# Bounded gathers and dealt-out rows in the expert stage of a one-core transformer kernel

## The reference

```python
g_gate, g_idx = lax.top_k(softmax(xf @ w_rg), 1)             # 1 of 4 groups
e_w, e_i = lax.top_k(softmax(e_logits_of_that_group), 2)     # 2 of its 8 experts
weights = g_gate * (e_w / sum(e_w))
# rows are sorted by expert and padded to whole blocks; for each block of rows:
hdn = silu(xb @ w1[e]) * (xb @ w3[e])
y   = hdn @ w2[e]
out = zeros.at[token].add(y * weight)                        # padding has weight 0
```

## Time and profile before

| | |
|---|---|
| median of 3 runs | 3100.24 us (3099.64 to 3101.42) |
| the profiled execution | 3102.82 us |
| its span in the trace | 3101.1 us |
| PE busy | 2788.8 us (90%) |
| DVE busy | 1741.9 us (56%) |
| ACT busy | 1243.8 us (40%) |
| POOL busy | 297.9 us (10%) |
| bytes moved by DMA | 509.35 MB |

### The profile page before, as it was taken

The page is one execution under the profiler, slowest core; times in us unless marked ns, Lnnn a source line. Parts: engine busy times, 40 slices in busy tenths (PEclk is TensorE's granted clock), DMA queues, the critical chain, the costliest instruction groups (busy, mean ns, idle before and its releaser), DMA issues. The chain is left out here.

```text
span 3101.1 us, 60598 instructions
## 1 busy us (share of the span) xinstructions
PE 2788.8 (90%) x24014; PEld 2191.8 (71%) x24014; DVE 1741.9 (56%) x3273; ACT 1243.8 (40%) x2039; POOL 297.9 (10%) x459
## 2 busy tenths in 40 slices
PE   7999896999769999999698999878888999978888
PEld 6787664777648877777476888755567888865557
DVE  4762777776151222222255677478965667559874
ACT  4332564885130100000164422268842322248861
POOL 0000562000021222222100000000000000000000
PEclk9999998999889999999899999989889999979889
DMA  5222754212369999999864133441045223270024
GB/s 182 90 78 76 236 164 156 78 49 88 130 243 345 380 378 375 380 381 377 285 226 148 57 109 109 144 144 28 1 138 168 69 88 109 87 221 14 14 82 142
DMA packets 226423, 509.35 MB, mean 164 GB/s; under 512 B 29216, under 2 KB 101728, under 8 KB 201536
## 3 DMA queue, kind: packets, MB, share of 16 engines
q1 hardware_dynamic: 202448, 448.57, 40.5%
q0 software_dynamic: 22640, 58.01, 6.8%
q10 hardware_dynamic: 1152, 0.27, 0.0%
HBM read 414.04 MB, written 93.66 MB: 164 GB/s over the span
## 5 line engine op out<-in xcount | busy, mean ns | idle before, releaser
L1933 PE MATMUL ps<-w_up,ex_xT 128*32 128x384 f32 x3072 | 344.0, 489 | 16.0 <-DMA w_up<-in_w_dram 15.0
L1935 PE MATMUL ps<-w_up,ex_xT 128*32 128x128 f32 x3072 | 348.0, 274 | 0.0
L1935 PEld LDWEIGHTS ps<-w_up,ex_xT 128*32 128x32 f32 x3072 | 330.9, 110 | 0.3
L1884 DVE TENSOR_TENSOR ex_hid<-ps,ex_act 32x128 f32<-32x128 f32 x96 | 28.2, 294 | 301.5 <-PE ps L1935 300.7
L927 ACT CAST next_w<-early 128x512 fp32r<-128x512 f32 x128 | 79.7, 623 | 256.6 <-PE ps L1245 219.4
L1960 PE MATMUL ps<-w_down,ex_hT 128*32 128x512 f32 (+1 forms) x1536 | 172.0, 487 | 8.6 <-DMA w_down<-in_w_dram 7.6
L1962 PE MATMUL ps<-w_down,ex_hT 128*32 128x256 f32 x768 | 172.2, 380 | 0.0
L1029 DVE TENSOR_TENSOR next_w<-early,next_w 128x512 fp32r<-128x512 f32 x128 | 88.3, 690 | 134.5 <-ACT next_w L927 133.7
L694 PE MATMUL ps<-mix_in_wh,mix_in_xh 128*128 128x512 f32 x384 | 152.4, 397 | 7.3 <-DVE mix_in_xl L474 3.7
L695 PE MATMUL ps<-mix_in_wl,mix_in_xh 128*128 128x512 f32 x384 | 150.6, 392 | 0.0
L696 PE MATMUL ps<-mix_in_wh,mix_in_xl 128*128 128x512 f32 x384 | 150.4, 392 | 0.0
(11 more groups left out here) (505 smaller groups left out, 7393.7 us busy)
## 6 DMA issues: line engine op xcount, KB each, us to landing
w_up<-in_w_dram SPq DMA_DIRECT2D x128, 1024.0 KB, 15.3
w_down<-in_w_dram SPq DMA_DIRECT2D x64, 1024.0 KB, 15.6
proj<-in_st SPq DMA_DIRECT2D x104, 256.0 KB, 2.1
da_w_ada<-in_w_ada_dram SPq DMA_DIRECT2D x32, 768.0 KB, 4.4
in_right<-in_w_in_dram SPq DMA_DIRECT2D x16, 1024.0 KB, 6.0
early<-in_w_in_dram SPq DMA_DIRECT2D x14, 1024.0 KB, 6.0
x<-proj SPq DMA_DIRECT2D x24, 512.0 KB, 6.2
proj<-mix_in_out SPq DMA_DIRECT2D x40, 256.0 KB, 2.0
```

Source lines behind the costliest of these rows:

```text
L1933: pe.matmul(o[group(g), :], tokens[g], wh[j][:, q, 0:HM], start=first, stop=end)
L1935: last = pe.matmul(o[BR:P, g * HQ:(g + 1) * HQ], tokens[g], wh[j][:, q, HM:], start=first and g == 0, stop=end, skip_group_check=True)
```

## The change

The table's padding triples get the token index 1024 instead of 0, which lies past the last row of `xn`. The gather gets a bound of 1023 and an instruction not to treat an index beyond it as an error, so that such rows are left alone. As a padding slot of `xg` then keeps what an earlier block left there, DVE clears `xg` once at the start of the phase, and POOL waits for that ahead of the first gather.

The slot of a row within its block changes too. Rank r within the block goes to slot 6 * (r mod 16) + floor(r / 16), so the rows are dealt out over 16 groups of 6 slots each. In the router DVE does this with two divisions with remainder (`divide`, four operations each) and two operations that join the parts, the second of which writes the integers for both choices at once. The two casts fall away, and `slots_done` is signalled once behind all of it. The scatter is not bounded and keeps its 96 rows.

```diff
+SPREAD = 16
+TO_WHOLE = 1.5 * 2.0 ** 23
-        slot_f = s.sb("slot_f", [P, NT])
+        slot_f, whole, part = (s.sb(n, [P, TOP_K, NT]) for n in ("slot_f", "whole", "part"))
...
             for i in range(TOP_K):
                 link(dve.tensor_tensor(mine[:], place[:], M[i][:], ALU.mult))
-                link(dve.tensor_reduce(slot_f[:], mine[:], X, ALU.add))
-                dve.tensor_copy(slot[:, i, :], slot_f[:]).then_inc(slots_done, 1)
-                dve.wait_ge(slots_done, i + 1)
+                link(dve.tensor_reduce(slot_f[:, i, :], mine[:], X, ALU.add))
+
+            def divide(to, of, by):
+
+                link(dve.tensor_scalar(to, of, 1.0 / by, (0.5 - by / 2) / by, ALU.mult, ALU.add))
+                link(dve.tensor_scalar(to, to, TO_WHOLE, None, ALU.add))
+                link(dve.tensor_scalar(to, to, -TO_WHOLE, None, ALU.add))
+                link(dve.scalar_tensor_tensor(out=of, in0=to, scalar=-float(by), in1=of, op0=ALU.mult, op1=ALU.add))
+
+            divide(whole[:], slot_f[:], BR)
+            divide(part[:], slot_f[:], SPREAD)
+            link(dve.scalar_tensor_tensor(out=part[:], in0=slot_f[:], scalar=float(BR // SPREAD), in1=part[:], op0=ALU.mult, op1=ALU.add))
+            dve.scalar_tensor_tensor(out=slot[:], in0=whole[:], scalar=float(BR), in1=part[:], op0=ALU.mult, op1=ALU.add).then_inc(slots_done, TOP_K)
+            dve.wait_ge(slots_done, TOP_K)
             weigh(1)
...
-        copied = s.sem("copied")
+        copied, emptied = s.sem("copied"), s.sem("emptied")
...
                 pool.indirect_dma_start(out=xg[:], out_offset=None, in_=k.xn[:, :],
-                                        in_offset=bass.IndirectOffsetOnAxis(ap=idx_own[:, 0:1], axis=0)).then_inc(gathered, 16)
+                                        in_offset=bass.IndirectOffsetOnAxis(ap=idx_own[:, 0:1], axis=0),
+                                        bounds_check=SEQ - 1, oob_is_err=False).then_inc(gathered, 16)
...
             load_row(0)
+            pool.wait_ge(emptied, 1)
             gather(0)
...
+            dve.memset(xg[:], 0.0).then_inc(emptied, 1)
             N2 = blocks_less_2(dve)
...
-    spares = np.stack([np.zeros(spare, int), SEQ + np.arange(spare) % P, np.zeros(spare, int)], 1).reshape(P, SPARE, 3)
+    spares = np.stack([np.full(spare, SEQ), SEQ + np.arange(spare) % P, np.zeros(spare, int)], 1).reshape(P, SPARE, 3)
```

## The result

The changed kernel takes 3084.40 us in the median of 5 runs (3082.31 to 3086.45), against 3100.24 us before: 15.8 us less, a ratio of 0.995 with a 95% interval of 0.9939 to 0.996. The profiled execution took 3082.31 us, its span is 3080.3 us.

A forecast was written before the change was run, and what follows sets the result against it. DMA engines were taken to bound the experts' stage, PE close behind. Skipped rows -10.5, router +1.8 and clearing 0 gave -8.7 us: 3091.5 us from 3100.2, range 3085.5 to 3103.5.

The forecast's parts named there:

- What bounds the stage: Experts' stage: DMA engines set 18.72 us a block, PE alone 17.64, leaving 23 us to gain before PE binds.
- The argument from the DMA share: Experts' stage: a DMA share of 1.01 to 1.02 was read as engines at their limit.
- Which rows go: Gathers of blocks 2 to 31 and the 33rd: 1069 rows leave while DMA binds, 66.8 per engine on average.
- rows aren't really skipped: Rival on the gather: out-of-range rows still cost a transfer, gain 0 to a third, 3102 or 3098.5 us; chance 0.20.
- The price of a row: Gather: a row costs an engine 0.175 us, at most 0.217 with the idx packets counted in.
- The fullest engine: Weight loads follow the engine with most rows kept; it loses 54 rows, 9.5 us, against 11.7 for the average.
- the HBM side binds: Loads in the experts' stage: if HBM were the limit, only bytes would count, 11.5 us gained.
- The tail: After 1510 us DMA engines aren't full; the last w2 wait of 2.84 us stays.
- The router's chain: DVE steps from first `mine` to weigh(1) grow from 2.25 to 4.04 us, 1.8 us lost, all on the path.
- POOL's later writes: Router: POOL's table writes start 2.9 us later but stay hidden before the barrier, counted as 0.
- Clearing xg and the bounded issue: Start of the experts' phase: clearing, new wait and first bounded gather together cost 0, bounds -0.3 to +1 us.
- the rival with slow gathers: Bounds checks in software make each gather dearer, so PE waits for xg every block: about 3130 us; chance 0.08.

The follow-up runs named there:

- e4: The changed kernel with the gather's bound at 0, so every gathered row but token 0's is left out (output not the reference's): 3074.24 us, ratio 0.9906.
- v3: The changed kernel with the scatter bounded too and a row's group rotated by the block number: 3076.08 us, ratio 0.9924 to the kernel before.
- e5: The changed kernel, but only padding slots with slot mod 6 = 5 are out of bounds, the others read row 0: 3092.35 us, ratio 0.9972.
- e9: Against e2, every gathered row has 768 numbers instead of 1024 (output not the reference's): 3085.36 us, ratio 0.9958 to the kernel before.
- e1: The kernel before with bounded gather, padding index 1024 and cleared xg, but rows in their old order, padding last: 3103.21 us, ratio 1.0009.
- e6: The changed kernel with a row's group rotated by the block number: 3084.84 us, ratio 0.9948 to the kernel before.
- e2: The changed kernel with padding index 0 and an unbounded gather, so rows are dealt out but none left out: 3103.15 us, ratio 1.0008.
- e8: e2 run once more without change: 3103.53 us, ratio 1.0006 to the kernel before.
- e10: Against e2, only the scatter is bounded, the gather stays whole: 3090.10 us, ratio 0.9968 to the kernel before.
- v1: The changed kernel with the scatter bounded as well as the gather: 3081.47 us, ratio 0.9935 to the kernel before.
- v1b: v1 run once more without change: 3079.11 us, ratio 0.994 to the kernel before.

## Why the prediction was right or wrong

- **What bounds the stage: right.** PE's pace of 17.64 us was read off the first blocks, and e4 and v3 run at it throughout. The room of 23 us that I gave before PE takes over was of the right size (from before to e4: 571.1 - 544.3 = 27 us). The argument from the DMA share was weak, though: e4 shows 101% without any wait.
- **Which rows go: right.** 1120 rows, 4.6 MB; the page shows exactly that. That rows aren't really skipped was wrong as a rival: they stay as packets, but cost next to nothing of the queue's own time (in e4's stretch above 145 small packets took 1.0% of 8.5 us, less than 0.1 us).
- **The price of a row: the step that failed.** I took 0.175 us, the weights' rate, and put the remaining 0.25 us of the queue's time down to the idx packets. That reading of the earlier trace rows was wrong: the small packets took 0.05 us and the rows 0.21 us each, next to my upper bound of 0.217. The price in the pace of the stage is higher still, 0.31 to 0.34 us (e5; e9 per 4 KB), so the step from the queue's own time to the time of the stage, one for one, failed as well. My 54 rows at 0.32 would have been 17 us; 18.0 were measured.
- **The fullest engine: right in kind, and it is what makes the deal matter.** e1 shows that skipping without it brings nothing. That only the fullest engine counts may be too strict, by e6. The Trainium skill's rule that I weighed there ("DMA: Bandwidth & Descriptors", section "Why a DMA increments its semaphore by 16 and not by 1", a transfer over 96 partitions is cut into 16 shares) fits e1. The other rule that I took from this page of the Trainium skill, in its note on 436, 358 and 368, that the HBM side binds, is not borne out. e1 moves fewer bytes than the kernel before, at 370 GB/s, and is no faster, and v3 moves 384 GB/s. The section "Measured (HBM→SBUF, 128 partitions, SWDGE, issued from GpSimd)" of that page of the Trainium skill gives about 358 GB/s to a core when both cores of the pair stream, which I left out; here one core runs.
- **The deal's own cost: missing from the sum.** I priced the deal only in the router. It also costs 3 us in the stage (e2, e8), cause unknown. So the gain over the dealt kernel is 18.0 us up to the 33rd gather, and 14.6 over the kernel before. Had the price been right, this missing term alone would have put the forecast 3 us too low.
- **The tail: wrong by 1.2 us.** I said it stays; it went from 40.81 to 39.63 us (40.42 and 39.69 in the second traces).
- **The router's chain: right.** +1.73 us of steps (forecast 1.8), and PE's wait before its tile grew by the same 1.73, from 2.86 to 4.59 us. The chain happens to begin 0.34 us earlier in this trace (886.08 against 886.42), so the tile starts 1.39 us later and the first gather 1.42. Counted from the first `mine`, the first gather comes 38.55 us later instead of 36.79, 1.76 us more, as forecast. POOL's later writes were hidden, as forecast.
- **Clearing xg and the bounded issue: right.** The memset takes 0.91 us, from 919.80, ahead of POOL's first load; the bounded gather's issue takes 1.03 us instead of 0.95, so the rival with slow gathers had nothing.
- **The range** was too narrow below because its low end used 0.217 us as the dearest row. The queue's share bounded what that queue spends; what leaving rows out was worth to the stage was half as much again.

In the sum: -10.5 should have been -14.6 up to the 33rd gather (-18.0 for the rows, +3.4 for the order), and -1.2 in the tail; with +1.4 that is -14.4 at the last scatter, against -8.7 forecast. The 1.4 us that the medians show beyond it lie in the rest of the span, whose spread is larger.

## What to carry to other kernels

If a transfer is cut over several engines and another waits for all of them, trimming it can pay only when every engine gets its part of the trim: deal the live rows out before you leave the dead ones out, and vary the remainder from block to block (2 us here). Price a small transfer beside a saturating one by taking a known amount of it away, since its own share of the queue left out a third of the price here. Before you put a part of a share down to small packets, cut the window so that they stand alone. And to tell which side is the bound, look at the pace of the loop and at how long a load takes to land, not at the busy share of the DMA engines.

## What the runs showed of the hardware

- A bounded gather's row that is out of range remains a packet of under 512 bytes (226423 packets before and after, 1120 more of them small), and the issue takes 1.03 us instead of 0.95. The scatter's issue stays at 1.49 us.
- Left out only at the end of each block, 1120 rows brought nothing (e1); dealt out over the 16 groups of six slots, 18.0 us against the dealt kernel with all rows.
- 4 KB rows gathered beside weight loads cost 0.31 to 0.34 us of the pace per row and engine, by bytes and not by packets (e9), where the queue's own time is 0.21 and the weights' rate gives 0.17 for the same bytes. Scattered rows with an addition cost about as much (e10).
- The DMA engines' shares add up to 101% in e4, where no load is waited for and loads land after 8.7 us, and to 102% in the kernel before, where they land after 15.4 us.
- Near the point where PE and the DMAs are equally fast, the same program (v1, v1b) gave stages of 595.0 and 588.5 us; the three others that ran twice repeated within 0.6 us.
- Open: why the dealt order costs 3 us with the same bytes, and skipping in the old order about as much; why a row costs more of the pace than its own time on the queue; and why the even deal brings less than the fullest engine's rows would ask for.
